# Joined two-half products in a chunked linear-attention scan, with the outputs' products behind the state steps

## What is computed

```python
def rwkv_step(S, inp):
    r, w, k, v, a, b = inp
    sa = jnp.einsum('bdhvk,bdhk->bdhv', S, a)
    S = S * w[..., None, :] + sa[..., None] * b[..., None, :] + v[..., None] * k[..., None, :]
    return S, jnp.einsum('bdhvk,bdhk->bdhv', S, r)
...
    xs = (both_directions(prep['r'], False),
          both_directions(prep['decay'], True),
          both_directions(prep['k_dir'], True),
          both_directions(prep['v'], False),
          -both_directions(prep['kk'], False),
          both_directions(prep['kk'][:, :, None] * prep['iclr'], True))
...
    state_ctx, yc = rwkv_scan(state0, prep_c)
    _, yx = rwkv_scan(state_ctx, prep_x)
```

## Time and profile before

| | |
|---|---|
| runs | 2538.64, 2541.12, 2541.31 us |
| profiled execution | 2535.24 us, its span 2533.4 us |
| TensorE busy | 2013.9 us, 79% |
| VectorE busy | 1661.4 us, 66% |
| ScalarE busy | 853.6 us, 34% |
| GpSimd busy | 680.0 us, 27% |
| mean granted TensorE clock | 0.92 |

### The profile page before, as it was taken

How to read it: one execution, slowest core, us unless ns; L and a number is a source line. 1 busy time by engine, 2 the same in 40 slices (tenths; PEclk the granted TensorE clock), 3 DMA queues, 4 the chain that set the end, 5 groups by cost and what they waited for, 6 DMA issues and landing times.

```text
span 2533.4 us, 40846 instructions
## 1 busy us (share of the span) xinstructions
PE 2013.9 (79%) x16281; PEld 1230.6 (49%) x16281; DVE 1661.4 (66%) x3506; ACT 853.6 (34%) x1682; POOL 680.0 (27%) x577
## 2 busy tenths in 40 slices
PE   5999947888678788887899887777777777778877
PEld 3766635666667776575455432333333333333332
DVE  4699964687034344554776777777777777777764
ACT  4666633465434343223223222222222121212121
POOL 0000020000112121002344445444444444444441
PEclk8999978988689999898999999999989999988999
DMA  6477653523443231436999999999999999999995
GB/s 240 155 254 250 224 204 143 186 72 117 176 166 140 104 137 45 169 117 242 421 420 415 383 420 416 420 421 419 421 419 421 420 421 419 421 420 421 421 421 214
DMA packets 136029, 742.01 MB, mean 293 GB/s; under 512 B 17920, under 2 KB 25120, under 8 KB 69280
## 3 DMA queue, kind: packets, MB, share of 16 engines
...
q10 hardware_dynamic: 1152, 2.10, 0.2%
...
## 4 chain that ended last, share of the span: by engine, by line
DMA 30%; PE 15%; DVE 4%; issue 3%; ACT 2%; POOL 0%; DVEq 0%; ACTq 0%
DMA uv<-in_uv_in,ic 30%; PE bank L2654 13%; DVE junk L2539 2%; DMA scores_dram<-later 1%; PE bank L92 1%; PE bank L94 1%; PE bank L93 1%; ACT dg L2451 1%; PE bank L2635 1%; POOL uv L2374 0%; DVE wql L2503 0%; ACT ge L2446 0%; ACT L2446 0%; DVE gc_ L2544 0%; ACT L2291 0%
## 5 line engine op out<-in xcount | busy, mean ns | idle before, releaser
L2654 PE MATMUL bank<-uv,dg 128*128 128x512 f32 x1664 | 816.1, 648 | 212.2 <-ACT dg L2451 212.1
L2654 PEld LDWEIGHTS bank<-uv,dg 128*128 128x128 f32 x1664 | 335.4, 206 | 682.8 <-issue 404.3
L2374 POOL DMA_INDIRECT uv<-in_uv_in,ic x416 | 478.2, 1150 | 627.8 <-PE bank L2654 556.5
L2539 DVE SCALAR_TENSOR_TENSOR junk<-uv,gr 128x1024 f32<-128x1024 f32 x416 | 510.1, 1226 | 185.7 <-DMA uv<-in_uv_in,ic 158.1
L2446 ACT ACTIVATE ge<-dt_ 128x4 f32<-128x4 f32 (+1 forms) x130 | 26.7, 205 | 945.1 <-DVE junk L2539 945.0
L2654 PE MATMUL bank<-uvx,dg 128*128 128x512 f32 x384 | 185.7, 641 | 52.5 <-ACT dg L2451 52.5
L2451 ACT ACTIVATE dg<-ident,gc_ 128x128 f32<-128x128 f32 x512 | 163.9, 390 | 31.2 <-DVE gc_ L2544 29.1
L2539 DVE SCALAR_TENSOR_TENSOR junk<-uvx,gr 128x1024 f32<-128x1024 f32 x96 | 117.7, 1226 | 58.6 <-DMA uvx<-in_uv_in,ic 56.0
L2654 PEld LDWEIGHTS bank<-uvx,dg 128*128 128x128 f32 x384 | 76.4, 204 | 161.7 <-issue 90.1
L2374 POOL DMA_INDIRECT uvx<-in_uv_in,ic x96 | 114.5, 1193 | 120.8 <-PE bank L2654 110.4
L92 PE MATMUL bank<-hx_hi,wzh 128*128 128x512 f32 x160 | 70.5, 440 | 34.9 <-DVE wzl L984 19.4
...
## 6 DMA issues: line engine op xcount, KB each, us to landing
...
uv<-in_uv_in,ic POOLq DMA_INDIRECT x416, 28.1
```

What stands on the lines that cost most here:

```text
L2374: pool.indirect_dma_start(ring(i), None, g["uv_in"], bass.IndirectOffsetOnAxis(ap=ic[:, s % ICR, k:k + 1], axis=0)).then_inc(su[row_slot[i ...
L2539: dve.scalar_tensor_tensor(junk[:, :], ring(i)[:, 0:D], 1.0, hc[:, t % 2, :], ALU.mult, ALU.mult, accum_out=dt[:, k:k + 1]).then_inc(s_ud, 1)
L2654: mm = pe.matmul(acc(t, c)[:, :], dg[:, n % 2, k, :], ring(i)[:, D + 512 * c:D + 512 * c + 512], start=h == 0 and q == 0 and k == 0, stop= ...
```

## The change

Keys and removal keys lie side by side in the record and in SBUF (`kb`: for each couple of chunks k, b, b, k), are stored and loaded as one field, and decayed by GpSimd direction by direction. With this one product of 128 weight columns does what two did in `products` 1 and 3. The turned keys and the masked products share a tile (`kr`), values and weighted values another (`vp`), each with one half of the partitions for the keys' side and the other for the removal keys' side, so that `updates` and `outputs` sum over 128 partitions in one product. `weighted` writes its output to the other half, which ScalarE takes out in three copies. The transitions of context chunks have a product of their own; those of latent chunks are joined with `carried` to 128 columns, in two parts.

In the order: `outputs` comes in two halves behind steps 1 and 2, `turned` and the gating behind step 2, `own` 0 and 1 at step 7, and the turns of keys behind them at steps 8 to 10. v is loaded after turn 12.

```diff
-                        sp.wait_ge(s_k, 2 * j)
-                        stored("k", j - 1)
...
+                        sp.wait_ge(s_k, 2 * j)
                         sp.wait_ge(s_b, 2 * j)
-                        stored("b", j - 1)
+                        stored("kb", j - 1)
...
-                        dve.tensor_tensor(rk[:, d, :, :], chunks(kf[:, d, :]), chunks(ei[:, d, :]), ALU.mult).then_inc(s_k, 1)
+                        dve.tensor_tensor(rk[:, d, :, :, :], pairs(kf[:, d, :]), pairs(ei[:, d, :]), ALU.mult).then_inc(s_k, 1)
...
-                    for i, o in enumerate((RC_A, RC_B)):
-                        sp.dma_start(ab[:, j % 2, i, :, :, :], record[j, :, o:o + NDIR * T].rearrange(
-                            "p (d c s) -> p d c s", d=NDIR, c=NC)).then_inc(s_ab[j % 2], 16)
+                    sp.dma_start(ab[:, j % 2, 0, :, :, :], record[j, :, RC_A:RC_K].rearrange(
+                        "p (d c s) -> p d c s", d=NDIR, c=NC)).then_inc(s_ab[j % 2], 16)
+                    sp.dma_start(ab[:, j % 2, 1, :, :, :].rearrange("p d (c w) s -> p (d c) (w s)", w=2), record[j, :, RC_K:RC_V].rearrange(
+                        "p (e w s) -> p e (w s)", w=4, s=CHUNK)[:, :, CHUNK:3 * CHUNK]).then_inc(s_ab[j % 2], 16)
...
-        lk, lb, la, lv = (sb(st, "l" + n, [P, NDIR, NC, CHUNK]) for n in ("k", "b", "a", "v"))
...
+        kb = sb(st, "lkb", [P, NDIR, NC // 2, 4, CHUNK])
+        var = sb(st, "lvar", [P, 4, NDIR, NC, CHUNK])
+        lv, la = var[:, 0, :, :, :], var[:, 1, :, :, :]
+        lr = (var[:, 2, :, CC:NC, :], var[:, 3, :, CC:NC, :])
+        dkb = var[:, 0:2, :, :, :].rearrange("p q d c s -> p (q d c s)").rearrange("p (d c w s) -> p d c w s", d=NDIR, c=NC // 2, w=4)
...
+        kr = sb(st, "kbt_rkb", [P, NE, 2, 2, 2, CHUNK])
+        vp = sb(st, "vt_pw", [P, NE, 2, 2, CHUNK])
...
+        pa = sb(st, "pw_a", [P, NE, 2, CHUNK])
...
-                            sp.wait_ge(s_t, 12 * (j - 1) + 9)
-                        sp.dma_start(lv[:, :, :, :], field(j, RC_V)).then_inc(s_lv, 16)
+                            sp.wait_ge(s_t, 12 * j)
+                        sp.dma_start(lv, field(j, RC_V)).then_inc(s_lv, 16)
...
+                    for d in range(NDIR):
+                        if d:
+                            pool.wait_ge(s_t, 12 * j + 6)
+                            pool.wait_ge(s_a, 2 * NR * j + 2 * NR)
+                        else:
+                            pool.wait_ge(s_t, 12 * j + 3)
+                        wide = e[:, d, :].rearrange("p (c w) -> p c w", w=2).unsqueeze(3).broadcast_to((P, NC // 2, 2, CHUNK))
+                        for w in (slice(0, 4, 3), slice(1, 3)):
+                            pool.tensor_tensor(dkb[:, d, :, w, :], kb[:, d, :, w, :], wide, ALU.mult).then_inc((s_kp, s_bp)[d], 1)
...
+                    src = bank[2 + n % 3][:, :].rearrange("p (e h k) -> p e h k", e=4, h=2)
+                    if n < 3:
+                        for p in range(2):
+                            act.activation(vp[HALF[p], 4 * n:4 * n + 4, p, :, :], src[HALF[p], :, :, :], ACT.Copy).then_inc(s_tc, 1)
+                    elif n < 6:
+                        act.activation(ra[:, 4 * (n - 3):4 * (n - 3) + 4, :, 1, :], src, ACT.Copy).then_inc(s_tc, 1)
+                    else:
+                        d, m = divmod(n - 6, 3)
+                        src = bank[2 + n % 3][:, :].rearrange("p (e c h k) -> p e c h k", e=2, c=2, h=2)
+                        for i in range(2):
+                            act.activation(kr[:, 4 * m + 2 * i + d, :, :, 0, :], src[:, i, :, :, :], ACT.Copy).then_inc(s_tc, 1)
...
-                    act.activation(pw[:, 2 * r:2 * r + 2, :, :, :], bank[2 + r % 3][:, :].rearrange(
-                        "p (e h q k) -> p e h q k", e=2, h=2, q=2), ACT.Copy).then_inc(s_pwc, 1)
+                    src = bank[2 + r % 3][:, :].rearrange("p (e h q k) -> p e h q k", e=2, h=2, q=2)
+                    for p in range(2):
+                        act.activation(vp[HALF[1 - p], 2 * r:2 * r + 2, p, :, :], src[HALF[1 - p], :, :, 0, :], ACT.Copy).then_inc(s_pwc, 1)
+                    act.activation(pa[:, 2 * r:2 * r + 2, :, :], src[:, :, :, 1, :], ACT.Copy).then_inc(s_pwc, 1)
...
+                        dve.wait_ge(s_m, 6 * j + p + 1)
+                        o = mt[:, p:CC:2, :, :]
+                        dve.tensor_tensor(o, bank[(2, 5)[p]][:, 0:HEAD * CC].rearrange("q (c d v) -> q c d v", c=CC // 2, d=2), o,
+                                          ALU.add).then_inc(s_mc, 1)
...
+                            dve.wait_ge(s_m, 6 * j + 2 * r + p + 3)
+                            src = bank[MG[r][p]][:, :].rearrange("p (c d w) -> p c d w", c=2, d=2)
+                            o = mt[:, c0 + p:c0 + 4:2, :, :]
+                            dve.tensor_tensor(o, src[:, :, :, 0:HEAD], o, ALU.add).then_inc(s_mc, 1)
+                            for d in range(NDIR):
+                                own = lr[j % 2][:, d, 4 * r + p:4 * r + 4:2, :]
+                                dve.tensor_tensor(gg[:, p, 2 * r:2 * r + 2, d, :], src[:, :, d, HEAD:], own[:, :, ::-1] if d else own,
+                                                  ALU.add).then_inc(s_gc, 1)
...
+                        cp, d = divmod(NE - NL + 4 * (n // 2) + x, 2)
+                        for p in range(2):
+                            for h in range(2):
+                                o = CHUNK * (2 * x + p)
+                                mm = pe.matmul(bank[h][:, o:o + CHUNK], kb[HALF[h], d, cp, 2 * p:2 * p + 2, :].rearrange("p q s -> p (q s)"),
+                                               lr[j % 2][HALF[h], d, 2 * cp + p - CC, :], start=True, stop=True)
+                                if x == 3 and p == 1:
...
-                        for lhs, rhs, q in ((kt, vt[:, e, :, :], 0), (bt, pw[:, e, :, 0, :], 1)):
+                        for p in range(2):
                             for h in range(2):
-                                for p in range(2):
-                                    mm = pe.matmul(bank[p][HALF[h], HEAD * x:HEAD * x + HEAD], lhs[HALF[p], e, h, :], rhs[HALF[p], h, :],
-                                                   start=q == 0, stop=q == 1)
-                                    if x == 2 * n - 1 and q == 1 and h == 1:
-                                        mm.then_inc(s_n, 1)
-                    if r:
-                        pe.wait_ge(s_mc, 4 * j + 2)
-                    for x in range(2 * n):
-                        e = 2 * c0 + x
+                                mm = pe.matmul(bank[p][HALF[h], HEAD * x:HEAD * x + HEAD], kr[:, e, p, h, 0, :], vp[:, e, p, h, :],
+                                               start=True, stop=True)
+                            if x == 2 * n - 1:
+                                mm.then_inc(s_n, 1)
+
+                def transitions(j):
+                    for x in range(CC):
                         for h in range(2):
                             for p in range(2):
-                                mm = pe.matmul(bank[2 + p][HALF[h], HEAD * x:HEAD * x + HEAD], pw[HALF[p], e, h, 1, :],
-                                               bt[HALF[p], e, h, :], start=True, stop=True)
-                                if x == 2 * n - 1 and h == 1:
+                                mm = pe.matmul(bank[(2, 5)[p]][HALF[h], HEAD * x:HEAD * x + HEAD], pa[HALF[1 - p], x, h, :],
+                                               kr[HALF[1 - p], x, p, h, 0, :], start=True, stop=True)
...
+                                mm = pe.matmul(bank[MG[r][p]][HALF[h], P * x:P * x + P], pa[HALF[1 - p], e, h, :],
+                                               kr[HALF[1 - p], e, p, h, :, :].rearrange("p q k -> p (q k)"), start=True, stop=True)
...
+                                    e += NE - NL
+                                    o = P * cp + HEAD * h
+                                    pe.matmul(bank[6 + r][HALF[p], o:o + HEAD], kr[:, e, r, h, 1, :], vp[:, e, r, h, :],
+                                              start=cp == 0 and h == 0, stop=False, skip_group_check=True)
...
                     updates(j, 0)
+                    transitions(j)
+                    carried(j, 0)
                     updates(j, 1)
-                    carried(j)
-                    outputs(j)
-                    if j:
-                        turned(j - 1)
+                    carried(j, 1)
                     for c in range(1, NC - 1):
                         step(j, c)
+                        if c < 3:
+                            outputs(j, c - 1)
+                        if j and c == 2:
+                            turned(j - 1)
                         if j == NPAIR - 1:
                             ahead(c - 1)
                         if j < NPAIR - 1:
-                            if c < 5:
+                            if c <= NR:
                                 products(j + 1, c - 1)
-                            if c == 1:
-                                turn(j + 1, 0)
```

(14 more changed lines are left out.)

250 lines of the change are left out of this document (113 added, 137 removed).

## The result

| kernel | median us | runs | profiled execution us |
|---|---|---|---|
| before | 2539.88 | 4, 2536.24 to 2541.31 | 2535.24 |
| after | 2511.87 | 4, 2508.57 to 2516.92 | 2514.67 |

The ratio is 0.9894, 95% interval 0.9871 to 0.9917. The forecast was 2528, a gain of 13; the gain is 28, about twice that. The time lies in the range, 3 us inside its low end. A second set of six runs of the same kernel, further down, gave 0.9904 (0.9886 to 0.9921), a gain of 26.6.

A forecast was written before the change was run, and what follows sets the result against it. TensorE was taken to bound the head-pair stage, a seventh of each period being issue waits. Seven periods -15.4, last pair -1.5, first pair +1, inversion +3: -12.9, from median 2541.12 to 2528 us; range 2509 to 2546 (some 0.8).

The forecast's parts named there:

- 1. Fewer instructions: TensorE's instruction stream in the head-pair stage: 804 records a pair for 1092 cut issue waits, -5.0 us a pair.
- rival B: Issue waits stay, not being the instruction stream or blocks taking over 4.3 us: 2566 us, chance 0.10 in full.
- 2. The middle: Each pair's stretch before its first state step: shorter without issue waits, despite a new VectorE wait, -1.2 us a pair.
- rival D: 3.2 us bare before step 1 for 1.3, ScalarE or VectorE late: 2541; chance 0.17 together with half of rival B.
- 3. The steps: Each pair's state steps: outputs and former pair's transposes moved in, tile changes and mask wait added, +3.1 us a pair.
- 4. Odd products: Products 1 and 3 with 128 weight columns: both halves load at once, 0.7 us more each, +1.4 a pair.
- Rivals A: Odd products cost what they did: 2518 us; chance 0.22 together with fewer waits still.
- C: Rival: the halves of odd products load weights in turn, 1.7 us more for each of 14, 2552; chance 0.08.
- 5. The clock: TensorE's half clock in the head-pair stage: most follows long waits, so 0.5 us a pair is taken back.
- The last pair: Last head pair, without next products: saves its own three fetch waits, pays the moved waits, -1.5 us (0 to -3).
- 6. Ahead of the scan: Inversion stage reading removal keys in 512 B pieces, +3 us; first pair's larger key load less a wait, +1.
- the missed store: Project stage's joined store of keys and removal keys, 20 us before they are rewritten: charged nothing.

## Why the prediction came out half as large as the gain

*1. Fewer instructions*: right. -5.0 forecast, -4.6 measured, as means over eight pairs (over the seven alone 6.4 and 1.6, so -4.8), and the multiples of 127 records show the cause, which rules out rival B. In the kernel before, this speaks against the rule of the Trainium skill (Runtime: NRT & Kernel Launch, "Instruction fetch mechanics") that crossings are mostly hidden: 6.0 us a pair weren't.

*2. The middle*: mechanism right, size wrong. Clean -2.6 for -1.2. Of the 1.4 too much, 0.8 is the weighted products with own 2 (6.75 for 5.97: I saw the output's new half and not that it frees own 2's quadrants), and most of the rest the double charge: updates 0 at 64 x 34 ns + 0.15 = 2.3 where 2.0 is measured, updates 1 at 1.3 for 1.1. The 34 ns behind them was taken from 64x64 tiles in the first place; joined 128x64 records take 29. The bare 1.25 before step 1 came as said; so rival D falls.

*3. The steps*: +3.1 forecast. The measured +2.8 of the clean steps holds part 4's 1.7, so this part took +1.1 (or +1.5, if part 4 is given the 1.3 us by which splitting shortens the steps). Outputs (2 x 1.08) and the turn (0.6) were sized right. Four changes of tile (0.6) were charged twice over. The mask wait stayed at 0.54 and didn't grow by 0.5; the trailing 0.2 of ScalarE didn't show; and a wait of 0.4 for the mask `ka`, ahead of products 1, went, since outputs 1 and the former turn now stand in front of it.

*4. Odd products*: 0.84 more each for 0.7, +1.7 for +1.4 (+1.3 net of the mask wait). Rivals A and C fall. The formula 32 x 107 / 2 = 1.71 was right and lacked only its own change of tile: 1.86 with it, for 1.94.

*5. The clock*: forecast -0.5 a period. Mean period less clean time less issue waits is 38.5 - 35.5 - 1.4 = 1.6 in after, 42.5 - 35.3 - 6.0 = 1.2 before. In seven periods half clock cost 0.04 x 269.6 = 10.8 us after and 0.04 x 297.4 = 11.9 before (both clocks 0.96): nothing that shows was given back. The 1.6 and 1.2 are all that is left over, half clock in the main; in after 0.2 of it is the one wait of 1.48 for ScalarE's `nn` in pair 1.

A period: -5.0 - 1.2 + 3.1 + 1.4 - 0.5 = -2.2 forecast; -4.6 - 2.6 + 1.1 + 1.7 + 0.4 = -4.0 measured. **The terms that failed are parts 2 and 3, too large by 1.4 and 2.0 us a pair**, 24 in seven. The issue waits (0.4), the odd products (0.3) and what is left over, the clock's part (0.9), took half of it back, which leaves the 12.4 us by which the seven periods fell short of the forecast. The last pair brought -3.4 for -1.5.

*6. Ahead of the scan*: +4 forecast (3 for the inversion, 1 for the first pair), +8 measured, and not where it was charged. Pair 0's first weighted product is 10 us later in the first profile. In the 13 profiles of after and its variants (two of them with the store cut) it lies at 697 to 705 us, once at 691.9, 699.5 on the mean, against one profile of before at 691.4. So +8 with a doubt of some 5. The first inversion products, before and after, and those of the fourth pair after the earlier trace rows:

```profile
430.67 2.84 PE L1383 MATMUL bank<-xb 64*64 64x64 f32 x96 [10.18 <-DMA xb<-pair_record]
```

```profile
438.06 2.84 PE L1385 MATMUL bank<-xb 64*64 64x64 f32 x96 [10.85 <-DMA xb<-pair_record]
...
457.02 1.16 PE L1385 MATMUL bank<-xb 64*64 64x64 f32 x62 [0.56 <-DMA xb<-pair_record]
```

The mean of the 13 less the one profile of before, stretch by stretch:

| stretch | us | least and most of the 13 |
|---|---|---|
| up to the last removal keys | +2.5 | -0.2 to +6.7 |
| from there to the pools' start | +1.4 | +0.9 to +1.7 |
| from there to the first inversion product | +1.7 | +1.4 to +1.9 |
| to the last product of the inversion that reads `xb` | +0.1 | -0.5 to +0.5 |
| from there to pair 0's first weighted product | +2.5 | -1.9 to +6.4 |

So the inversion itself, which I charged with 3, is as long as before, pieces of 512 B or not: products of pairs two to four waited 2.5 us for loads in the first profile, 1.5 before, and that was made up. What was missed are 3.1 us around the pools, there in all 13: the missed store's 1.4, and 1.7 before the first inversion product, of which the wait for its first load shows 0.7 (10.85 for 10.18). Why is open; I ran nothing that takes the loads of 512 B back. The first and the last row scatter by 7 and 8 us from one profile to the next, so a single profile of before can't tell them from nothing.

The profiles differ by 20.6 us, 7.7 more than the 12.9 forecast: 12.4 in the seven periods and 1.9 in the last pair, less 6.0 ahead of the scan and 0.6 behind it. The medians differ by 28.0. The 7.4 between the two is chance in the executions: before's profile was 4.6 below its median, after's 2.8 above. So half of the 15 us by which the gain was missed is mechanism and half is which execution was profiled.
